# A hybrid encoder block with expert retrieval: U and V gathered as one row of 8 KB, weights formed two rows at a time

## The reference

```python
def peer_ffn(h, w_q, sub_keys, u_tab, v_tab):
    q = (h @ w_q).reshape(Bb, S, PEER_HEADS, 2, PEER_HALF)
    scores = jnp.einsum('bshpd,pnd->bshpn', q, sub_keys)
    vals, idx = lax.top_k(scores, PEER_TOPK)                  # 16 of 128, twice, per head
    cand = vals[..., 0, :, None] + vals[..., 1, None, :]      # 256 sums
    cidx = idx[..., 0, :, None] * PEER_NKEYS + idx[..., 1, None, :]
    top_vals, pos = lax.top_k(cand, PEER_TOPK)
    eidx = jnp.take_along_axis(cidx, pos, axis=-1)            # 16 experts per head, 8 heads
    gates = jax.nn.softmax(top_vals, axis=-1)
    u = jnp.take(u_tab, e, axis=0)
    act = jax.nn.gelu(jnp.einsum('td,thkd->thk', xt, u))
    vv = jnp.take(v_tab, e, axis=0)
    return jnp.einsum('thk,thkd->td', g * act, vv)
```

## Time and profile before

| | us |
|---|---|
| runs | 3883.16, 3861.61, 3858.42; median 3861.61 |
| profiled execution | 3826.47 |
| its span | 3824.7 |
| busy PE, DVE, POOL, ACT | 2919.9, 2603.0, 2337.5, 893.9 |

### The profile page before, as it was taken

One profiled execution on the slowest core, in us unless ns is written; L12 is line 12 of the kernel. 1 busy time (PEld: TensorE's weight loads), 2 busy tenths in 40 slices (PEclk: granted clock), 3 DMA queues, 4 the chain that ended last, 5 costly groups with the idle time before them and its releaser, 6 DMA issues.

```text
span 3824.7 us, 34537 instructions
## 1 busy us (share of the span) xinstructions
PE 2919.9 (76%) x11088; PEld 1913.1 (50%) x11088; DVE 2603.0 (68%) x5403; ACT 893.9 (23%) x1935; POOL 2337.5 (61%) x2052
## 2 busy tenths in 40 slices
PE   8989888568877787788877787867676676667777
PEld 6868657455534464655544454634443443324224
DVE  1144888996677857876768867877668767863541
...
DMA  6657999899999999899999999899999999997995
GB/s 220 221 203 263 388 356 379 313 403 388 382 412 364 381 371 382 318 382 385 385 375 394 389 387 376 342 369 406 395 408 377 412 412 411 399 367 277 397 373 203
DMA packets 342549, 1373.44 MB, mean 359 GB/s; under 512 B 38737, under 2 KB 40657, under 8 KB 309730
## 3 DMA queue, kind: packets, MB, share of 16 engines
q0 software_dynamic: 294912, 1073.87, 72.9%
q1 hardware_dynamic: 47458, 297.36, 19.8%
...
...
## 4 chain that ended last, share of the span: by engine, by line
PE 16%; POOL 15%; issue 9%; DMA 7%; DVE 3%; another core or an unknown queue 2%; ACT 2%; ACTq 0%; DVEq 0%; POOLq 0%
POOL ubuf L431 8%; POOL vbuf L431 7%; PE ysum L673 7%; DMA vbuf<-in_v,idx 5%; PE bank L488 4%; PE bank L497 3%; DMA ubuf<-in_u,idx 1%; DVE ubuf L1133 1%; PE bank L660 1%; ACT diag L885 1%; DVE acc L1159 0%; PE bank L553 0%; DVE tX L1055 0%; PE wide L505 0%
## 5 line engine op out<-in xcount | busy, mean ns | idle before, releaser
L431 POOL DMA_INDIRECT ubuf<-in_u,idx x1024 | 1175.4, 1148 | 1054.0 <-DVE ubuf L1133 535.2
L673 PE MATMUL ysum<-vbuf,diag 128*128 128x512 f32 x2048 | 1157.2, 708 | 685.3 <-DMA vbuf<-in_v,idx 322.4
L1133 DVE SCALAR_TENSOR_TENSOR ubuf<-ubuf,hbuf 128x1024 f32<-128x1024 f32 x1024 | 1246.8, 1222 | 416.4 <-DMA ubuf<-in_u,idx 339.9
L431 POOL DMA_INDIRECT vbuf<-in_v,idx x1024 | 1161.9, 1135 | 381.7 <-issue 294.0
L673 PEld LDWEIGHTS ysum<-vbuf,diag 128*128 128x128 f32 x2048 | 416.2, 219 | 1309.3 <-issue 923.9
L1159 DVE SCALAR_TENSOR_TENSOR acc<-vbuf,dots,acc 128x1024 f32<-128x1024 f32 x505 | 645.5, 1278 | 62.0 <-DMA vbuf<-in_v,idx 38.5
L488 PE MATMUL bank<-hT,slab 128*128 128x256 f32 (+1 forms) x3680 | 674.5, 343 | 12.1 <-DMA slab<-in_slabs 4.9
L488 PEld LDWEIGHTS bank<-hT,slab 128*128 128x128 f32 x3680 | 601.0, 195 | 118.0 <-issue 55.2
L497 PE MATMUL bank<-slab,hT 128*128 128x256 f32 x1408 | 316.2, 384 | 1.1 <-ACT rE L700 0.8
L497 PEld LDWEIGHTS bank<-slab,hT 128*128 128x128 f32 x1408 | 271.4, 193 | 57.7 <-issue 21.6
L885 ACT ACTIVATE diag<-ident,dots 128x128 f32<-128x128 f32 x512 | 189.6, 394 | 370.3 <-PE ysum L673 148.7
...
## 6 DMA issues: line engine op xcount, KB each, us to landing
slab<-in_slabs SPq DMA_DIRECT2D x255, 1024.0 KB
ubuf<-in_u,idx POOLq DMA_INDIRECT x1024
vbuf<-in_v,idx POOLq DMA_INDIRECT x1024
rX<-in_x SPq DMA_DIRECT2D x6, 1024.0 KB, 8.6
hbuf<-x_d SPq DMA_DIRECT2D x8, 512.0 KB
tX<-x_d SPq DMA_DIRECT2D x8, 512.0 KB, 10.4
out<-tX SPq DMA_DIRECT2D x8, 512.0 KB
x_d<-rX SPq DMA_DIRECT2D x3, 1024.0 KB, 4.5
```

The costliest lines, as they stand in the source:

```text
L431: nc.gpsimd.indirect_dma_start(out=dst, out_offset=None, in_=rows, in_offset=bass.IndirectOffsetOnAxis(ap=idx[:, b, k:k + 1], axis=0)).the ...
L673: ins = mm(ysum[:, c, :], diag[:, m % DS, :], vbuf[:, at % VS, c * 512:c * 512 + 512], start=(m == first), stop=(m == last))
L1133: v.scalar_tensor_tensor(out=row, in0=row, scalar=1.0, in1=hbuf[:, i % 2, :], op0=ALU.mult, op1=ALU.mult, accum_out=dots[:, g % 3, k:k + 1 ...
```

## The change

- The host joins the tables into one of 16384 rows of 8 KB. POOL issues 1024 gathers into `uv`, a ring of ten slots (80 KB of each partition, before 56). The first half of a slot is dotted, the second added; a slot is freed by the add alone.
- The add follows the dot by one step on DVE and two on PE, in place of ten. ACT makes a gelu of two dots in each step (before 16 dots in each eighth), and DVE multiplies two dots with two shares; `shares` does the softmax's division ahead, two instructions to a head.
- PE takes the odd rows of tiles 1 to 7, but none of the first six of a tile. It does them between the halves of a front stage (`add_rows`) instead of ahead of it. ACT does the stage of n - 1 in step n.
- `acc` is two buffers that start as x1; X2 goes to DRAM and is read back for the tail. The normed token goes to DRAM once and is read as `hbuf`. `tX`, `probs`, `pT`, `otok` and the regions rX to rE are replaced by shared buffers that a segment and a tail use in turn, with waits for the transfers that free them; `g_ffn` is loaded in each segment, the next segment's x only after `wq8`, and gates and branches go through rings of two.
- The window attention's stages are chained and mixed with gates; a segment with a guest tail has its stages `T0` to `T2` between `wq2` and `wq8`. The tail of tile 6 alone lies in tile 7.

```diff
-US, VS, DS = 6, 8, 3
+DS = 3
...
+NS = 10
+HB = 2
 STEPS = TOPK // 2
-VLAG = STEPS + 2
-UEND = NHEAD * STEPS
-VEND = UEND + VLAG
+ROWS = NHEAD * TOPK
+END = NHEAD * STEPS
+PER_TILE = NH * STEPS
 AHEAD = 2 * STEPS
 
 
 ODD = tuple(range(1, TOPK, 2))
-ON_PE = [(), ODD, ODD, ODD, ODD, ODD, ODD, tuple(range(TOPK))]
-ROWS = UEND * 2
-IS_PE = [at % TOPK in ON_PE[at // (NH * TOPK)] for at in range(ROWS)]
+ON_PE = [(), ODD, ODD, ODD, ODD, ODD, ODD, ODD]
+SPARE = 6
+IS_PE = [at % TOPK in ON_PE[at // (NH * TOPK)] and at % (NH * TOPK) >= SPARE for at in range(ROWS)]
...
+GROUPS = ((0, 1), (2, 3), (4, 5), (6,), (7,))
+HOST = {0: 2, 1: 3, 2: 4}
...
-        ubuf = sb("ubuf", [P, US, D])
-        vbuf = sb("vbuf", [P, VS, D])
-        hbuf = sb("hbuf", [P, 2, D])
-        acc = sb("acc", [P, D])
+
+        uv = sb("uv", [P, NS, 2 * D])
+        hbuf = sb("hbuf", [P, HB, D])
+        acc = sb("acc", [P, 2, D])
...
+                if at == 1 and n == "bgs3":
+
+                    sp.wait_ge(bank_full, USES_END[s, "bgs3"])
+                    sp.dma_start(x1[:, 0:SEGS[s], :], x_rows(s)).then_inc(xres_in, 16)
+                if at == 2 and n == "swo3":
+                    sp.wait_ge(vec_done, VEC_ORDER[s, "swo3"])
+                    sp.dma_start(g_ffn, a["g_ffn"].partition_broadcast(P)).then_inc(gffn_in, 16)
...
+                if at == 2 and n == "rt":
                     sp.wait_ge(vec_done, VEC_ORDER[s, "rt"])
+                    sp.dma_start(tiles(h_d, s), h2[:, 0:SEGS[s], :]).then_inc(h_out, 16)
+                if at == 1 and n == f"wq{NH}" and s + 1 < NSEG:
+                    sp.wait_ge(bank_full, USES_END[s, n])
                     sp.dma_start(xs[:, 0:SEGS[s + 1], :], x_rows(s + 1)).then_inc(x_in, 16)
...
+            for n in range(FIRST, LAST + 3):
+                i, at = divmod(n + 10, PER_TILE)
                 if at == 0 and 0 <= i < NTILE:
 
                     sp.wait_ge(x1_out, 16 * (seg_of(i) + 1))
                     if i >= 2:
-                        sp.wait_ge(u_used, (i - 1) * NH * TOPK)
-                    sp.dma_start(hbuf[:, i % 2, :], x1_d[i]).then_inc(h_in, 16)
-                i, at = divmod(n - 62, UEND // NTILE)
+                        sp.wait_ge(x2_out[i % 2], 16 * (i // 2))
+                    sp.dma_start(acc[:, i % 2, :], x1_d[i]).then_inc(acc_in[i % 2], 16)
+                i, at = divmod(n + (10 if HB > 1 else 0), PER_TILE)
                 if at == 0 and 0 <= i < NTILE:
 
-                    if i >= 2:
-                        sp.wait_ge(tail_out[i % 2], 16 * (i // 2))
-                    sp.dma_start(tX[:, i % 2, :], x1_d[i]).then_inc(tX_in[i % 2], 16)
-                for at in range(4):
+                    sp.wait_ge(h_out, 16 * (seg_of(i) + 1))
+                    if i >= HB:
+                        sp.wait_ge(dot_done, (i - HB + 1) * NH * TOPK)
+                    sp.dma_start(hbuf[:, i % HB, :], h_d[i]).then_inc(h_in[i % HB], 16)
+                i, at = divmod(n - 3, PER_TILE)
+                if at == 0 and 1 <= i <= NTILE:
+                    sp.wait_ge(x2_done, i)
+                    sp.dma_start(x2_d[i - 1], acc[:, (i - 1) % 2, :]).then_inc(x2_out[(i - 1) % 2], 16)
...
+            for at in range(ROWS):
+                g, k = divmod(at, TOPK)
+                if k == 0:
+                    pool.wait_ge(idx_ready, g + 1)
+                if at >= NS:
+                    if IS_PE[at - NS]:
+                        pool.wait_ge(v_used_pe, PE_UPTO[at - NS + 1])
+                    else:
+                        pool.wait_ge(v_used_dve, DVE_UPTO[at - NS + 1])
                 nc.gpsimd.indirect_dma_start(
-                    out=dst, out_offset=None, in_=rows,
-                    in_offset=bass.IndirectOffsetOnAxis(ap=idx[:, b, k:k + 1], axis=0)).then_inc(done, 16)
-
-            for n in range(0, VEND):
-                for at in (2 * n, 2 * n + 1):
-                    if n < UEND:
-                        g, k = divmod(at, TOPK)
-                        if k == 0:
-                            pool.wait_ge(idx_ready, g + 1)
-                        if at >= US:
-                            pool.wait_ge(u_used, at - US + 1)
-                        gather(a["u"], ubuf[:, at % US, :], g % 4, k, u_in[at % US])
-                for at in (2 * (n - VLAG), 2 * (n - VLAG) + 1):
-                    if n >= VLAG:
-                        g, k = divmod(at, TOPK)
-                        if at >= VS:
-                            if IS_PE[at - VS]:
-                                pool.wait_ge(v_used_pe, PE_UPTO[at - VS + 1])
-                            else:
-                                pool.wait_ge(v_used_dve, DVE_UPTO[at - VS + 1])
-                        gather(a["v"], vbuf[:, at % VS, :], g % 4, k, v_in[at % VS])
+                    out=uv[:, at % NS, :], out_offset=None, in_=a["uv"],
+                    in_offset=bass.IndirectOffsetOnAxis(ap=idx[:, g % 4, k:k + 1], axis=0)
+                    ).then_inc(uv_in[at % NS], 16)
...
             def by_feature(src, tt):
                 w = next_piece()
+                for gs in feature_banks(tt):
+                    b = bank_for()
+                    for g in gs:
+                        if g:
+                            add_rows()
+                        o = b[:, (g - gs[0]) * tt * P:(g - gs[0] + 1) * tt * P]
+                        for k in range(KT):
+                            m = mm(o, w[:, k, g * P:g * P + P], src(k), start=(k == 0), stop=(k == KT - 1))
...
+                if n not in PIECES or n in ("glo0", "swo0", "wo0", "wq0", "pg0"):
+                    add_rows()
...
+                rows_due += [at for at in (2 * (n - 2), 2 * (n - 2) + 1) if 0 <= at < ROWS and IS_PE[at]]
                 for s, name in AT_STEP.get(n, []):
                     stage(s, name)
                     assert used.n == USES_END[s, name], (s, name)
+                add_rows()
...
+            def gelu(n):
+                g, at = divmod(n, STEPS)
+                part = dots[:, g % 3, 2 * at:2 * at + 2]
+                act.wait_ge(dot_done, 2 * n + 2)
+                fn(part, part, ACT.Gelu_apprx_tanh).then_inc(gelu_done, 1)
...
+                for at in (2 * (n - 2), 2 * (n - 2) + 1):
+                    if 0 <= at < ROWS and IS_PE[at]:
+                        diagonal(at)
+                if 0 <= n - 1 < END:
+                    gelu(n - 1)
                 g, at = divmod(n, STEPS)
-                if at == 0 and 1 <= g <= NHEAD:
-                    gelu(g - 1)
                 if at == 4 and 0 <= g + 2 < NHEAD:
                     peer_exp(g + 2)
-                for s, name in AT_STEP.get(n, []):
+                for s, name in AT_STEP.get(n - 1, []):
                     stage(s, name)
...
+                dve.wait_ge(uv_in[at % NS], (at // NS + 1) * 16)
+                row = uv[:, at % NS, 0:D]
+                v.scalar_tensor_tensor(out=row, in0=row, scalar=1.0, in1=hbuf[:, i % HB, :], op0=ALU.mult, op1=ALU.mult,
+                                       accum_out=dots[:, g % 3, k:k + 1]).then_inc(dot_done, 1)
+
+            def shares(m, j):
+
+                if j == 0:
+                    dve.wait_ge(topk_exp, m + 1)
+                    v.reciprocal(ginv[:, m % 2, :], gsum[:, m % 4, :]).then_inc(share_step, 1)
+                else:
+                    dve.wait_ge(share_step, 2 * m + 1)
+                    v.tensor_scalar(gexp[:, m % 4, :], gexp[:, m % 4, :], ginv[:, m % 2, :], None, ALU.mult
+                                    ).then_inc(share_step, 1)
+
+            def weights(n):
+
+                g, at = divmod(n, STEPS)
+                part = slice(2 * at, 2 * at + 2)
+                dve.wait_ge(gelu_done, n + 1)
+                dve.wait_ge(share_step, 2 * g + 2)
+                v.tensor_tensor(dots[:, g % 3, part], dots[:, g % 3, part], gexp[:, g % 4, part], ALU.mult
+                                ).then_inc(wts_done, 1)
 
             def add_row(at):
                 g, k = divmod(at, TOPK)
                 i = g // NH
                 m = DVE_UPTO[at]
-                first = DVE_UPTO[i * NH * TOPK]
-                dve.wait_ge(wts_step, 2 * (g + 1))
+                dve.wait_ge(wts_done, at // 2 + 1)
                 if m:
                     dve.wait_ge(v_used_dve, m)
-                if m == first and i:
-                    dve.wait_ge(x2_done, i)
-                dve.wait_ge(v_in[at % VS], (at // VS + 1) * 16)
-                weight = dots[:, g % 3, k:k + 1]
-                if m == first:
-                    ins = v.tensor_scalar(acc[:], vbuf[:, at % VS, :], weight, None, ALU.mult)
-                else:
-                    ins = v.scalar_tensor_tensor(out=acc[:], in0=vbuf[:, at % VS, :], scalar=weight, in1=acc[:],
-                                                 op0=ALU.mult, op1=ALU.add)
-                ins.then_inc(v_used_dve, 1)
+                if m == DVE_UPTO[i * NH * TOPK]:
+                    dve.wait_ge(acc_in[i % 2], 16 * (i // 2 + 1))
```

(77 more changed lines are left out.)

498 lines of the change are left out of this document (240 added, 258 removed).

## The result

The changed kernel takes 3680.3 us (median of four runs, 3679.6 to 3681.6) where the kernel before takes 3860.0 beside it: ratio 0.953 [0.948, 0.957]; the brackets hold the 95% interval. Repeated in a later session it took 3678.8 for 3829.0: 0.961 [0.958, 0.963]. Medians and ratios are of fast executions alone: one of e4 (9788 us) and one of e9 (3890 us) are left out as slow. I had predicted 3817 with a low end of 3690. The profiled span went from 3824.7 to 3679.7 us.

What follows compares the result with a forecast made beforehand. DMA bounds the kernel, POOL second. Front +10, tile 0 +30, tiles 1 to 6 -23, later X loads +8, tile 7 -46, end -23: sum -44 on 3824.7, span 3781, by ratio 3817; range 3690 to 3980.

Steps and rivals of the forecast that it cites:

- lock-step rival: Tiles 0 to 7: each weight instruction waits for its rows' gelu on ACT, 206 us slower, by ratio 4025; chance 0.20.
- some 300 for front stages: Tiles 1 to 6: DVE's waits for front stages, some 300 us, kept unchanged in the sum after the change.
- hidden under DMA with 271 us: Tiles 1 to 6: DVE's extra work, about +60 us, stays under the transfers with 271 us spare, 0.7 us a step.
- Packets: Gathered rows, tiles 1 to 6: one 8 KB packet is 1.6% cheaper than two of 4 KB, 30 us less.
- cut rows: All gathers: each 8 KB row becomes two descriptors, +11 us, 3836, by ratio 3873; chance 0.13.
- POOL's relief: Tiles 1 to 6: halving POOL's gathers gives back 20 us of lost transfer time, bounds 0 and 60.
- 352 us for tile 7: Tile 7: 46 us less, from 341 of transfers plus 11 of loss as in tile 6, bounds 330 and 385.
- Ceiling: Tiles 0 to 6: POOL starved DMA, search bursts (50) and tile 0 (20) recover; -154 us, by ratio 3706; chance 0.17.
- ring: Gather slots, held until the add, rule if PE's row is over 8 us late: 0.3 us a row, +230; chance 0.06.
- Front: Before tile 0: the late load of the next X costs 9 us, chained gates 1; together 10 us longer.
- tile 0: Tile 0 has no cover for DVE's earlier adds (26 us) and weights (35); 30 us longer, bounds 10 and 60.
- end: After the last dot: 57 us for 80, 23 less; X2's store and load 5.3 each, then 38.6 + 2.

Runs made afterwards that it cites:

- e4: The kernel after with eight gather slots in place of ten: 3748.0 us, ratio 0.978 to the kernel before.
- e9: The kernel before with half of tile 7's rows on DVE, not all on PE: 3852.4 us, ratio 1.001.
- e17: The kernel before with ACT's front stage one step later than PE as its only change: 3761.9 us, ratio 0.983.
- e7: The kernel after with ACT's front stages back in PE's own step: 3753.4 us, ratio 0.973 to the kernel before.
- e1: The kernel after with each slot filled by two gathers of 4 KB rows: 3784.3 us, ratio 0.981 to the kernel before.
- e16: The kernel after with two memsets (128x1024 and 128x640) on POOL behind each gather: 3791.6 us, ratio 0.989 to the kernel before.
- e14: The kernel after with all rows of tile 7 but the first six on PE: 3684.6 us, beside 3678.8 for the kernel after.
- e2: The kernel after with one memset of 128x1024 on POOL behind each gather: 3680.2 us, ratio 0.955 to the kernel before.
- e18: The kernel after with two 4 KB gathers to a slot and ACT's front stages in PE's own step: 3843.6 us, ratio 1.004 to the kernel before.

## Why the prediction was wrong, step by step

**ACT's stage one step later: priced at nothing.** This is the step that failed: 72 us (e17), of the 137 by which I was off. (In the profiled spans it is 63 of 101; the kernel before ran 35 us faster when profiled than its median, and the kernel after did not.) The prediction names the move only inside the lock-step rival ("the new order gives ACT one step more") and keeps "some 300 for front stages" as it was. The rows were there: ACT's two largest waits for PE's banks, 45 of 9.8 us. I asked what they would do to the new gelu, not what they already did to the diagonals behind them and to DVE's parts of the front; PE's waits for `diag` I didn't look up, and DVE's 300 us I took for fixed. e17 shows the price without the rest of the change, e7 with it. By this, the argument "hidden under DMA with 271 us" was too coarse as well: those 271 us are a sum over six tiles, and e17 gained 61 us in them by shorter waits alone. That a wait costs transfer time at once when a slot comes free late by it fits e4 (two slots fewer cost 70 us); it was not measured wait by wait.

**Packets: right in kind, small in size.** The rival *cut rows* is false (147456 packets). The "1.6% cheaper" came from the mean time of the slabs' packets; the rate of undisturbed slices rose 2.4%, 47 us in tiles 1 to 6 for my 30. The page "DMA: Bandwidth & Descriptors" of the Trainium skill (section on SWDGE, HWDGE and iDMA) prefers packets of at most 4096 bytes; here gathered rows of 8192 went as one each, and faster. It states a preference; that longer rows would be cut was my reading.

**POOL's relief: looked for in the wrong place.** For tiles 1 to 6 I took 20 of 0 to 60; e1 leaves some 5 there (51.5 - 47) once packets are taken out, less than executions of e1 differ by (15 us). I sought it where POOL was 87% busy and DMA had other work too, and put nothing of it in tile 7, where POOL had to bring all the bytes alone: 353 GB/s stood there, and I laid it to PE. 2 x (1.14 + 0.29) us for a row is 367 GB/s. That division would have found it; e1 prices it at about 25 us of tile 7, e16 shows the limit by itself. The sum's 352 us for tile 7 came near 334.5 partly by luck: moving rows off PE, its main reason, was worth 5 us (e14) or none (e9); the smaller tail, its other one, is the likely source of some 26. Its "11 of loss as in tile 6" is misread too: tile 6 lost 6. The page "SBUF — State Buffer" of the Trainium skill (who interferes with whom) let me think that starved descriptors might be the ceiling. It has such an instruction of DVE hold off GpSimd's reads only, so the step to descriptors was mine; a gather of 8 KB rows takes 1.29 us on average, but e2 shows that POOL's time is free up to 2.43 us a row, so no run here supports a loss by it in tiles 1 to 6.

**Ceiling.** Its time (3706) was nearest, its cause wrong: the bursts gave next to nothing back (tiles 2 and 4 took 442 and 445 us after, 450 and 443 before), tile 0 nothing, and POOL's share of tiles 1 to 6 was some 5 us. That it came near is luck.

**Lock-step and ring.** Lock-step didn't occur: 68 us of waits for the gelu, under the 250 that I had set. Its mechanism is real (e7: 327 us), but costs 73 and not 206: 48 of the 64 that I had set for tile 0, 23 of 115 in tiles 1 to 6 and some 4 of 27 in tile 7. So the cover in tiles 1 to 6 was larger than I had it. The ring too is near its edge, but eight slots cost 2%, some 0.07 us a row, not the 0.3 that I had worked out for a slot held too long.

**Front, tile 0, end.** Front +24 for +10: PE idles in two places, where the batches of the attention part stand behind each other (38.5 us busy between 100 and 150 us, 45.8 before) and where the next X is late (a wait of 16.7 us on ACT's L840; before, 8.1). Which share each has no run tells. Tile 0 +11 for +30: within the bounds, but only by the move of ACT, which the sum didn't have; without it tile 0 is 60 us longer than before (e7, e18). The end, 50.4 for my 57: the load of x_d landed after 3.4 us, not 5.3, and what follows it took 37.5, not 40.6.
